# First guess of the inverse root in the stream norms: VectorE's reciprocal and a ScalarE square root in place of logarithm and exponential

## Chip, cores and metric

The kernel runs on one core of a Trainium2 chip. The metric is the device time of one execution in microseconds (us), lower is better. The time of the kernel before is the median of three runs, and its profile is one further execution.

## What is computed

Two transformer blocks follow each other on 512 tokens of width 1024, in fp32. The first has a gated feed-forward layer (ffn1), a mixer of gated linear attention and convolution (mix), a cross attention to a memory of 256 tokens (xat) and a second feed-forward layer (ffn2), and ends in a norm. The second adds 16 meta tokens (528 in all) and has a latent attention (mla), a feed-forward layer with convolution (cffn0), a pooling mixer (pool) and another such layer (cffn1). Ahead of each layer, and behind each of the second block, stands an RMS norm over the width:

```python
def rms_norm(x, g):
    xf = x.astype(jnp.float32)
    y = xf * lax.rsqrt(jnp.mean(xf * xf, axis=-1, keepdims=True) + EPS)
    return (y * g.astype(jnp.float32)).astype(x.dtype)
```

The change touches how `rsqrt` of that mean is found for twelve of these norms.

## The kernel before

The activations X lie with the width on the 128 partitions, as eight tiles of 128 x tokens. A weight matrix is read in units: a unit is up to eight tiles of 128x128, which SP loads (`raw`), ScalarE rounds into a high part (`w_hi`, L490), and GpSimd subtracts into a low part (`w_lo`, L477). PE multiplies the unit in three passes (L544 w_hi by high part of X, L546 w_hi by its low part, L548 w_lo by its high part) into one of four pairs of PSUM banks. There are four raw slots and two of w_hi and w_lo, so `w_hi` of unit n+2 waits until PE is through with unit n, and PE waits for the two halves of `w_lo` of its unit.

Each engine runs a program written out by hand in one order; semaphores join them, and there is no planner. A norm is made so. ScalarE squares the tiles (L639). They are summed over the tiles either on PE, which multiplies each by ones (`pe_square`, L566), or on VectorE (`acc`, L654) with one multiplication by ones at the end (`pe_norm`, L559). Every partition then holds the sum for every token, so the rest is work on a 128 x tokens tile (512, 516 or 528 tokens):

- VectorE, `dve_norm`: L688 scales and adds EPS, out of PSUM into `ms`, and signals `norm_ms`.
- ScalarE, `act_sqrt`: waits for `norm_ms`, then `act_rsqrt`: `sd = Ln(ms)` at L670, `sd = Exp(-0.5 sd)` at L671, signals `norm_sd`. Ahead of an activation whose table is not loaded stands an ACT_TABLE_LOAD, put down to the activation's line.
- VectorE waits for `norm_sd` and does one Newton step in three instructions (`newton`, L675 to L677), which gives `rn`.

`sd` and the scratch `rt` are slices of `post_t`, which is the name that the rows show. In `dve_norm` and `newton` `link` makes VectorE wait for its own last write.

```python
    def newton(link, r, v, t, s, last=None):
        link(nc.vector.tensor_tensor(t, s, s, ALU.mult))
        link(nc.vector.scalar_tensor_tensor(t, t, -0.5, v, ALU.mult, ALU.mult))
        (last or link)(nc.vector.scalar_tensor_tensor(r, t, 1.5, s, ALU.add, ALU.mult))
```

Twelve norms go through `act_sqrt` and `dve_norm`, here called by their places: FFN1, MIX, XAT, FFN2 (ahead of the layers of the first block), FIN (its end), MLA, MLAP (ahead of and behind the latent attention), CF0, CF0P, POOL, POOLP and CF1 (likewise around cffn0, pool and cffn1). Seven of them (FFN1, MIX, XAT, FFN2, MLA, CF0, CF1) stand ahead of a layer whose first product does not need `rn`: the weights are multiplied by X scaled by the gain alone, and `rn` comes in when the product is read out of PSUM (L903 in `dve_ffn`). PE goes on with units 1, 2 and 3 in that time; before unit 3 it waits for `norm_ms`, since that unit's PSUM pair held the sum. The other five (FIN, MLAP, CF0P, POOL, POOLP) make values that the next product needs (`dve_post`, L959 and L963: X plus the normed output; L1716; L2340 for the pool).

ScalarE's order at a feed-forward layer is: `w_hi` of unit 2, `act_sqrt`, then the first activations of the layer, then `w_hi` of unit 3. Eight further inverse roots (four in the mixer, one of the memory, two of the latent attention, one at the output) call `act_rsqrt` directly.

Of the kernel before, what the change touches and what calls it, by code (L numbers as in the profile page):

```python
# [17 lines left out]
ALU = mybir.AluOpType  # L18
ACT = mybir.ActivationFunctionType
# [3 lines left out]
D = 1024  # L23
# [12 lines left out]
EPS = 1e-6  # L36
# [106 lines left out]
def program(nc, ctx, A, out):  # L143
    def sb(name, shape, dt=F32, scope=ctx):
        return scope.enter_context(nc.sbuf_tensor(name, shape, dt))

    def sem(name):
        return ctx.enter_context(nc.semaphore(name))
# [12 lines left out]
    ms = sb("ms", [P, S2 + 8])  # L161
    rn = sb("rn", [P, S2 + 8])
    post_t = sb("post_t", [P, 3, S2 + 8])
    rt, sd = post_t[:, 0, :], post_t[:, 1, :]
# [125 lines left out]
    norm_ms = sem("norm_ms")  # L290
    norm_sd = sem("norm_sd")
# [213 lines left out]
    def psv(pair, blk):  # L505
        return PS[pair][:, 0, :] if blk == 1 else PS[pair][:, :, 0:width(blk) // 2]

    def sv(ap, blk):
        return ap if blk == 1 else ap.rearrange("p (c w) -> p c w", c=2)

    def width(blk):
        return (S1, S2, S3)[blk - 1]
# [142 lines left out]

    def act_sqrt(act, s, w):
        act.wait_ge(norm_ms, s + 1)
        act_rsqrt(act, sd[:, 0:w], ms[:, 0:w]).then_inc(norm_sd, 1)

    act_steps = [0]  # L660

    def act_link(act, ins):

        act_steps[0] += 1
        ins.then_inc(act_step, 1)
        act.wait_ge(act_step, act_steps[0])

    def act_rsqrt(act, dst, v):

        act_link(act, nc.scalar.activation(dst, v, ACT.Ln))  # L670
        return nc.scalar.activation(dst, dst, ACT.Exp, scale=-0.5)  # L671
# [7 lines that stand above are left out]
    def dve_norm(dve, link, s, pair, blk, rc=0):  # L679

        w = width(blk)
        if s in PE_SUMMED:
            dve.wait_ge(acc_done, KD * (s + 1))
        else:
            dve.wait_ge(norm_sum, len([x for x in range(s + 1) if x not in PE_SUMMED]))
        if rc:
            link(nc.vector.tensor_scalar(ms[:, w:w + rc], PS[pair][:, 1, 0:rc], 1.0 / D, EPS, ALU.mult, ALU.add))
        nc.vector.tensor_scalar(sv(ms[:, 0:w], blk), psv(pair, blk), 1.0 / D, EPS, ALU.mult, ALU.add).then_inc(norm_ms, 1)  # L688
        dve.wait_ge(norm_sd, s + 1)
        w += rc  # L690
        newton(link, rn[:, 0:w], ms[:, 0:w], rt[:, 0:w], sd[:, 0:w])

    def gain_of(name, index):
# [130 lines left out]
    def act_ffn(act, name, blk, inv, s, after):  # L824
# [4 lines left out]
        for pi, (f0, nt) in enumerate(PARTS):  # L829
# [9 lines left out]
            def up(it, n=n, pi=pi, f0=f0, count=count):  # L839
                for a in range(2):  # L840
                    g = (inv * FT + f0 + a) + 2 * it
                    soon = blk > 1 and first(it) and pi == 0 and a == 0
                    look(it, n, 2 * a, count)
                    if first(it) and pi == 0 and a == 0:
                        act_sqrt(act, s, w)
                    act.wait_ge(unit_read, later(n, it, 2 * a + 1))
                    if blk > 1:
                        f = (f0 + a) + 2 * it
                        nc.scalar.activation(g_conv[:, 0:w], g_buf[:, 2:2 + w], ACT.Identity, scale=tap(inv - 2, 2, f),  # L849
                                             bias=tap(inv - 2, 3, f)).then_inc(conv_tap, 1)  # L850
                        if soon:
                            look(it, n, 2 * a + 1, count)
                        act.wait_ge(conv_done, (2 * (cb + f0 + a) + 1) + 4 * it)
                        nc.scalar.activation(g_act[:, 0:w], g_conv[:, 0:w], ACT.Silu).then_inc(silu_done, 1)
                    else:
                        nc.scalar.activation(g_act[:, 0:w], g_buf[:, 0:w], ACT.Silu).then_inc(silu_done, 1)
                    if not soon:
                        look(it, n, 2 * a + 1, count)
                    if blk > 1:
                        act.wait_ge(unit_read, later(n, it, 2 * a + 2))  # L860
                        nc.scalar.activation(u_conv[:, 0:w], u_buf[:, 2:2 + w], ACT.Identity, scale=tap(inv - 2, 2, f + FT),  # L861
                                             bias=tap(inv - 2, 3, f + FT)).then_inc(conv_tap, 1)
                    act.wait_ge(hid_prod, g + 1)
                    nc.scalar.activation(h_hi[:, a + 2 * it, 0:w], hid[:, 0:w], ACT.Copy).then_inc(hid_hi, 1)  # L864
# [19 lines left out]
    def dve_ffn(dve, link, name, blk, inv, s, after):  # L884
# [3 lines left out]
        if blk > 1:  # L888
            link(nc.vector.memset(g_buf[:, 0:2], 0.0))
            link(nc.vector.memset(u_buf[:, 0:2], 0.0))  # L890
        dve_norm(dve, link, s, (n + 3) % 4, blk)
        r = sv(rn[:, 0:w], blk)
        n_down = None
# [59 lines left out]
    def dve_post(dve, link, i, s, n, gain, d_next=None, g_next=None, blk_next=2):  # L953
        dve_norm(dve, link, s, n % 4, 2)
        for k in range(KD + 3):
            if k < KD:
                if k >= 3:
                    dve.wait_ge(post_added, KD * i + k - 2)
                nc.vector.scalar_tensor_tensor(post_t[:, k % 3, 0:S2], M[:, k, :], gain(k), rn[:, 0:S2], ALU.mult,  # L959
                                               ALU.mult).then_inc(post_scaled, 1)  # L960
            if 1 <= k <= KD:
                dve.wait_ge(post_scaled, KD * i + k)
                nc.vector.tensor_tensor(X[:, k - 1, :], X[:, k - 1, :], post_t[:, (k - 1) % 3, 0:S2],  # L963
                                        ALU.add).then_inc(post_added, 1)
            if k >= 3 and d_next is not None:
                dve_split(dve, d_next, k - 3, blk_next, g_next)

    def act_post(act, i, s, s_next, d_next=None, g_next=None, blk_next=2):
        act_sqrt(act, s, S2)
        for k in range(KD):  # L970
            act.wait_ge(post_added, KD * i + k + 1)
            if d_next is not None:
                act_split(act, d_next, k, k, blk_next, g_next)
            act_square(act, s_next, k, k, xt(k, blk_next), width(blk_next))
# [232 lines left out]
    def act_mixer(act):  # L1207
# [3 lines left out]
        act.dma_start(gate_w[0:16, 0:256], A["gate_fwd_w"][0]).then_inc(small_in, 16)  # L1211
        act.dma_start(gate_w[16:32, 256:512], A["gate_bwd_w"][0]).then_inc(small_in, 16)
        act_sqrt(act, S_MIX, S1 + 4)
        hi_to(act, n + 4)
        pe_mix.wait(act, "lg")
# [96 lines left out]
    def dve_mixer(dve, link):  # L1312
# [9 lines left out]
        dve.wait_ge(unit_summed, n)  # L1322
        dve_mix.inc(nc.vector.memset(gate_w[:, :], 0.0), "gz")
        dve_norm(dve, link, S_MIX, (n + 3) % 4, 1, rc=4)
        nc.vector.tensor_tensor(zz[:, :], summed(0)[0:32, :], R[0:32, :], ALU.mult).then_inc(unit_read, 1)
        for t in range(2):
# [1160 lines left out]
```

## Time and profile before

| what | value |
| --- | --- |
| median of three runs | 2468.05 us (2458.19 to 2468.3) |
| the profiled execution: its time, and its span | 2468.25 us, 2466.5 us |
| busy: PE, VectorE, ScalarE, GpSimd | 94%, 43%, 37%, 40% |
| instructions of PE, VectorE, ScalarE | 14099, 1584, 1656 |
| L670 and L671, ACT_TABLE_LOAD | 20 and 20, 25.7 us each |

The span is from the first to the last instruction; the execution's own time has 1.75 us beside it. PE is busy nearly throughout, so time is won or lost where it stands still: such a place is read from the idle time ahead of an instruction of PE's timeline and the engine that ended it.

### The profile page before, as it was taken

To read this page: it belongs to the slowest core of one execution; us is meant where nothing else is said; L and a number is where in the kernel's file an instruction comes from. 1 tells how busy PE (TensorE), PEld (TensorE's weight loads), DVE (VectorE), ACT (ScalarE), POOL (GpSimd) and SP (SyncE) were. 2 spreads that over 40 slices of the span, in tenths; PEclk is the share of its full clock that TensorE was granted. 3 is DMA by queue.
4 is the path that set the end of the run, shared out by engine and by line. 5 is a ranking of instruction groups with operands and counts; after the bars stand their busy time and mean duration, and the time that the engine had idled before them with its cause. 6 is when DMAs were issued, how large, how long until landed. Compare 5 with 4: busy or idle time off the path is not lost.

```text
span 2466.5 us, 35997 instructions
## 1 busy us (share of the span) xinstructions
PE 2308.9 (94%) x14099; PEld 2027.3 (82%) x14099; DVE 1069.0 (43%) x1584; ACT 910.1 (37%) x1656; POOL 998.1 (40%) x758
## 2 busy tenths in 40 slices
PE   8999999999889899999988999799999938999999
PEld 6888887777677678888877888799999837999999
DVE  3313134564432242231356563562644475626354
ACT  4323235313353342222354453542433335424243
POOL 3445454532363344444531112244444432444443
PEclk9999999998899999999999999899999968999999
DMA  4333323321242123333211011133232201333221
GB/s 145 94 97 95 94 81 91 86 69 35 86 137 69 52 84 96 94 94 94 86 56 32 28 35 49 48 93 94 86 94 84 79 9 57 89 94 94 86 88 67
DMA packets 355686, 193.61 MB, mean 78 GB/s; under 512 B 7357, under 2 KB 350034, under 8 KB 355554
## 3 DMA queue, kind: packets, MB, share of 16 engines
q1 hardware_dynamic: 355026, 190.61, 26.4%
q8 instruction: 90, 1.47, 0.2%
q10 hardware_dynamic: 528, 1.19, 0.2%
q14 instruction: 42, 0.34, 0.0%
HBM read 189.67 MB, written 2.10 MB: 78 GB/s over the span
## 4 chain that ended last, share of the span: by engine, by line
PE 82%; DVE 11%; ACT 4%; issue 2%; DMA 0%; DVEq 0%; ACTq 0%; SPq 0%; POOL 0%
PE PS L544 22%; PE PS L546 22%; PE PS L548 22%; PE PS L1966 2%; PE PS L566 2%; PE PS L1984 1%; DVE u_conv L908 1%; PE PS L2038 1%; PE PS L2020 1%; ACT w_hi L490 1%; DVE g_conv L908 1%; PE PS L1155 1%; DVE hid L919 1%; PE PS L1567 1%; DVE u_conv L911 1%
## 5 line engine op out<-in xcount | busy, mean ns | idle before, releaser
L477 POOL TENSOR_TENSOR w_lo<-raw,w_hi 128x512 fp32r<-128x512 f32 (+4 forms) x743 | 976.4, 1336 | 1417.9 <-ACT w_hi L490 1417.9
L544 PE MATMUL PS<-XHI,w_hi 128*128 128x512 f32 (+2 forms) x2632 | 741.8, 332 | 41.0 <-DVE XLO L644 37.0
L490 ACT ACTIVATE w_hi<-raw 128x512 fp32r<-128x512 f32 (+4 forms) x743 | 412.5, 604 | 943.4 <-PE PS L548 879.4
L546 PE MATMUL PS<-XLO,w_hi 128*128 128x512 f32 (+2 forms) x2632 | 731.6, 328 | 0.0
L548 PE MATMUL PS<-XHI,w_lo 128*128 128x512 f32 (+2 forms) x2632 | 729.0, 327 | 0.0
L544 PEld LDWEIGHTS PS<-XHI,w_hi 128*128 128x128 f32 x2632 | 446.8, 190 | 97.4 <-issue 45.2
L546 PEld LDWEIGHTS PS<-XLO,w_hi 128*128 128x128 f32 x2632 | 444.7, 190 | 46.3 <-issue 2.9
L548 PEld LDWEIGHTS PS<-XHI,w_lo 128*128 128x128 f32 x2632 | 445.0, 190 | 43.6
L544 PE MATMUL PS<-h_hi,w_hi 128*128 128x512 f32 (+2 forms) x1056 | 282.3, 321 | 5.9 <-DVE h_lo L921 5.8
L546 PE MATMUL PS<-h_lo,w_hi 128*128 128x512 f32 (+2 forms) x1056 | 281.6, 321 | 0.0
L548 PE MATMUL PS<-h_hi,w_lo 128*128 128x512 f32 (+2 forms) x1056 | 281.5, 321 | 0.0
L544 PEld LDWEIGHTS PS<-h_hi,w_hi 128*128 128x128 f32 x1056 | 174.9, 188 | 23.7 <-issue 6.3
L546 PEld LDWEIGHTS PS<-h_lo,w_hi 128*128 128x128 f32 x1056 | 175.7, 189 | 16.1
L548 PEld LDWEIGHTS PS<-h_hi,w_lo 128*128 128x128 f32 x1056 | 175.1, 188 | 15.3
L903 DVE TENSOR_TENSOR u_buf<-PS,rn 128x512 f32<-128x512 f32 (+2 forms) x88 | 61.2, 695 | 229.7 <-PE PS L548 229.7
L864 ACT ACTIVATE h_hi<-hid 128x512 fp32r<-128x512 f32 (+5 forms) x88 | 56.0, 636 | 207.6 <-DVE hid L919 207.6
L903 DVE TENSOR_TENSOR g_buf<-PS,rn 128x512 f32<-128x512 f32 (+2 forms) x88 | 61.1, 694 | 99.2 <-PE PS L548 99.1
L936 DVE SCALAR_TENSOR_TENSOR X<-PS,X 128x512 f32<-128x512 f32 x48 | 33.2, 691 | 160.6 <-PE PS L548 160.6
L921 DVE TENSOR_TENSOR h_lo<-hid,h_hi 128x512 f32 (+5 forms) x88 | 68.9, 783 | 73.7 <-ACT h_hi L864 73.7
L908 DVE SCALAR_TENSOR_TENSOR u_conv<-u_buf,cols,u_conv 128x528 f32<-128x528 f32 (+1 forms) x44 | 71.4, 1622 | 65.7 <-ACT u_conv L861 65.7
L908 DVE SCALAR_TENSOR_TENSOR g_conv<-g_buf,cols,g_conv 128x528 f32<-128x528 f32 (+1 forms) x44 | 55.0, 1251 | 47.4 <-ACT g_conv L849 47.4
L2088 ACT ACTIVATE pt<-PS 128x640 f32<-128x640 f32 (+4 forms) x80 | 37.4, 472 | 87.0 <-PE PS L2020 86.1
(294 smaller groups left out, 2404.3 us busy)
## 6 DMA issues: line engine op xcount, KB each, us to landing
raw<-in_ffn_w_up SPq DMA_DIRECT2D x132, 512.0 KB, 3.7
raw<-in_ffn_w_down SPq DMA_DIRECT2D x64, 512.0 KB, 3.8
raw<-in_ffn_w_gate SPq DMA_DIRECT2D x44, 512.0 KB, 3.8
raw<-in_w_in SPq DMA_DIRECT2D x25, 512.0 KB, 3.7
raw<-in_ffn_w_down SPq DMA_DIRECT2D x32, 384.0 KB, 3.4
raw<-in_xattn_w_kv SPq DMA_DIRECT2D x16, 512.0 KB, 3.7
raw<-in_w_out SPq DMA_DIRECT2D x8, 512.0 KB, 3.7
raw<-in_xattn_w_q SPq DMA_DIRECT2D x8, 512.0 KB, 4.4
```

What stands on the lines that cost most here:

```text
L477: ins = nc.gpsimd.tensor_tensor(d, r, h.bitcast(F32), ALU.subtract)
L490: ins = nc.scalar.activation(d, r, ACT.Copy)
L544: nc.tensor.matmul(ps, wh, ahi(k)[:, c:c + w], start=(k == 0), stop=False)
L546: nc.tensor.matmul(ps, wh, alo(k)[:, c:c + w], start=False, stop=False)
L548: ins = nc.tensor.matmul(ps, wl, ahi(k)[:, c:c + w], start=False, stop=(k == u.kt - 1))
L566: ins = nc.tensor.matmul(ps, ones, sq[:, k % 2, c:c + w], start=(k == 0), stop=(k == KD - 1))
L864: nc.scalar.activation(h_hi[:, a + 2 * it, 0:w], hid[:, 0:w], ACT.Copy).then_inc(hid_hi, 1)
L903: nc.vector.tensor_tensor(sv(dst, blk), psv(m % 4, blk), r, ALU.mult).then_inc(unit_read, 1)
L908: nc.vector.scalar_tensor_tensor(cv_[:, 0:w], buf[:, 1:1 + w], tap(inv - 2, 1, ft), cv_[:, 0:w], ALU.mult, ALU.add).then_inc(conv_mid, 1)
L921: nc.vector.tensor_tensor(h_lo[:, a + 2 * it, 0:w], hid[:, 0:w], h_hi[:, a + 2 * it, 0:w].bitcast(F32), ALU.subtract).then_inc(hid_lo, 1)
L1966: ins = nc.tensor.matmul(bank[:, 0:CW], w, x[:, k, c * CW:(c + 1) * CW], start=st, stop=sp_)
L2088: act_m.inc(nc.scalar.activation(pt[:, x % 4, 0:j + 1, 0:nq], turn_at(x).rearrange("p (i q) -> p i q", q=P)[:, :, 0:nq], ACT.Copy), ("tc", x))
```

## The change

In `dve_norm` VectorE now follows the scaling at L688 with a reciprocal of `ms` into `sd`, and `norm_ms` is signalled by the reciprocal. In `act_sqrt` ScalarE takes the square root of `sd` in place, with one activation (L658), in place of `act_rsqrt`. The Newton step stays. The eight direct calls of `act_rsqrt` stay. Behind L655 lines shift by up to one, so L903 is now L904.

```diff
     def act_sqrt(act, s, w):
         act.wait_ge(norm_ms, s + 1)
-        act_rsqrt(act, sd[:, 0:w], ms[:, 0:w]).then_inc(norm_sd, 1)
+        nc.scalar.activation(sd[:, 0:w], sd[:, 0:w], ACT.Sqrt).then_inc(norm_sd, 1)
@@ dve_norm
         if rc:
             link(nc.vector.tensor_scalar(ms[:, w:w + rc], PS[pair][:, 1, 0:rc], 1.0 / D, EPS, ALU.mult, ALU.add))
-        nc.vector.tensor_scalar(sv(ms[:, 0:w], blk), psv(pair, blk), 1.0 / D, EPS, ALU.mult, ALU.add).then_inc(norm_ms, 1)
+        link(nc.vector.tensor_scalar(sv(ms[:, 0:w], blk), psv(pair, blk), 1.0 / D, EPS, ALU.mult, ALU.add))
+        w += rc
+        nc.vector.reciprocal(sd[:, 0:w], ms[:, 0:w]).then_inc(norm_ms, 1)
         dve.wait_ge(norm_sd, s + 1)
-        w += rc
         newton(link, rn[:, 0:w], ms[:, 0:w], rt[:, 0:w], sd[:, 0:w])
```

The order of instructions on ScalarE at the norms MLAP and CF0, of the kernel before (`XHI` is the high part of X, `sq` a squared tile; the eight pairs L633, L639 between the two norms are cut to the first). At MLAP:

```order
L639 ACTIVATE sq<-M 128x528
L670 ACT_TABLE_LOAD
L670 ACTIVATE post_t<-ms 128x528
L671 ACT_TABLE_LOAD
L671 ACTIVATE post_t<-post_t 128x528
L633 ACTIVATE XHI<-X,cols 128x528
```

At CF0:

```order
L490 ACTIVATE w_hi<-raw 128x512 x2
L670 ACT_TABLE_LOAD
L670 ACTIVATE post_t<-ms 128x528
L671 ACT_TABLE_LOAD
L671 ACTIVATE post_t<-post_t 128x528
L849 ACTIVATE g_conv<-g_buf,cols 128x528
```

The same two places in the changed kernel, MLAP first:

```order
L639 ACTIVATE sq<-M 128x528
L658 ACT_TABLE_LOAD
L658 ACTIVATE post_t<-post_t 128x528
L633 ACTIVATE XHI<-X,cols 128x528
```

```order
L490 ACTIVATE w_hi<-raw 128x512 x2
L658 ACTIVATE post_t<-post_t 128x528
L850 ACTIVATE g_conv<-g_buf,cols 128x528
```

The load and the activation between `ms` and the result are gone, and the second of two such norms in a row has no load at all. Over the whole program ScalarE has 48 table loads before and 33 after; two are new, ahead of the first exponential of the mixer's gates (L1226) and of the cross attention's softmax (L1611).

VectorE at MLAP in the changed kernel:

```order
L688 TENSOR_SCALAR ms<-PS 128x528
L690 RECIPROCAL post_t<-ms 128x528
L675 TENSOR_TENSOR post_t<-post_t 128x528
L676 SCALAR_TENSOR_TENSOR post_t<-post_t,ms 128x528
L677 SCALAR_TENSOR_TENSOR rn<-post_t 128x528
```

The reciprocal of the whole tile is new and stands behind L688, at all twelve norms; nothing else moves. PE, GpSimd and SP have the same instructions in the same order.

## Rows read from the trace of the kernel before

**Rows 1.** The page: span, and the chain that ended last, by engine.
```profile
span 2466.5 us, 35997 instructions
...
PE 82%; DVE 11%; ACT 4%; issue 2%; DMA 0%; DVEq 0%; ACTq 0%; SPq 0%; POOL 0%
```

**Rows 2.** PE's timeline at five norms: start us, length us, what [idle before <- releaser].
```profile
1254.27 0.56 PE L544 MATMUL PS<-XHI,w_hi 128*128 128x264 f32 x1 [8.01 <-DVE XLO L644]
1567.94 0.78 PE L544 MATMUL PS<-XHI,w_hi 128*128 128x264 f32 x2 [11.12 <-DVE XLO L644]
1979.59 0.78 PE L566 MATMUL PS<-sq,const 128*128 128x264 f32 x1 [8.52 <-ACT sq L639]
2018.28 0.56 PE L2259 MATMUL PS<-XHI,w_hi 128*128 128x264 f32 x1 [28.39 <-DVE XLO L2345]
2054.86 0.55 PE L544 MATMUL PS<-XHI,w_hi 128*128 128x258 f32 x1 [11.24 <-DVE XLO L644]
```

**Rows 3.** VectorE's timeline, the first Newton step of those five norms, same columns.
```profile
1249.63 0.69 DVE L675 TENSOR_TENSOR post_t<-post_t 128x512 f32<-128x512 f32 x1 [2.64 <-ACT post_t L671]
1974.47 0.71 DVE L675 TENSOR_TENSOR post_t<-post_t 128x528 f32<-128x528 f32 x1 [2.66 <-ACT post_t L671]
1993.36 0.71 DVE L675 TENSOR_TENSOR post_t<-post_t 128x528 f32<-128x528 f32 x1 [2.66 <-ACT post_t L671]
2047.16 0.71 DVE L675 TENSOR_TENSOR post_t<-post_t 128x528 f32<-128x528 f32 x1 [2.80 <-ACT post_t L671]
```

**Rows 4.** ScalarE's and VectorE's timelines at the norm behind the latent attention (MLAP).
```profile
1554.71 1.28 ACT L670 ACT_TABLE_LOAD   x1
1557.60 0.64 ACT L670 ACTIVATE post_t<-ms 128x528 f32<-128x528 f32 x1 [1.61 <-DVE ms L688]
1558.26 1.28 ACT L671 ACT_TABLE_LOAD   x1
1559.55 0.64 ACT L671 ACTIVATE post_t<-post_t 128x528 f32<-128x528 f32 x1
...
1556.86 0.71 DVE L688 TENSOR_SCALAR ms<-PS 128x528 f32<-128x528 f32 x1 [1.31 <-PE PS L559]
1560.23 0.71 DVE L675 TENSOR_TENSOR post_t<-post_t 128x528 f32<-128x528 f32 x1 [2.66 <-ACT post_t L671]
```

**Rows 5.** Groups of VectorE instructions, shapes kept apart: count, busy us, mean ns.
```profile
L675 DVE TENSOR_TENSOR post_t<-post_t 128x528 f32<-128x528 f32 x7 | 5.0, 708 | 17.9 <-ACT post_t L671 17.8
L675 DVE TENSOR_TENSOR post_t<-post_t 128x4 f32<-128x4 f32 x1 | 0.2, 151 | 0.0
L2167 DVE RECIPROCAL mst<-mst 128x1 f32<-128x1 f32 x80 | 12.5, 156 | 5.3 <-ACT pr L2079 4.3
L1679 DVE RECIPROCAL xst<-xst 128x1 f32<-128x1 f32 x16 | 2.5, 153 | 0.0
L919 DVE TENSOR_TENSOR hid<-g_act,u_buf 128x512 f32<-128x512 f32 x44 | 63.9, 1453 | 4.9 <-ACT g_act L856 0.3
```

**Rows 6.** Timelines at the latent norm (MLA): ScalarE, VectorE, GpSimd.
```profile
1280.99 1.15 ACT L490 ACTIVATE w_hi<-raw 128x512 fp32r<-128x512 f32 x2 [0.72 <-PE PS L548]
1273.48 0.71 DVE L675 TENSOR_TENSOR post_t<-post_t 128x528 f32<-128x528 f32 x1 [3.56 <-ACT post_t L671]
1278.32 2.54 POOL L477 TENSOR_TENSOR w_lo<-raw,w_hi 128x512 fp32r<-128x512 f32 x2 [6.69 <-ACT w_hi L490]
```

**Rows 7.** The same three engines at the first norm of the program (FFN1).
```profile
44.26 1.15 ACT L490 ACTIVATE w_hi<-raw 128x512 fp32r<-128x512 f32 x2 [1.81 <-PE PS L548]
37.34 0.69 DVE L675 TENSOR_TENSOR post_t<-post_t 128x512 f32<-128x512 f32 x1 [3.59 <-ACT post_t L671]
41.48 3.06 POOL L477 TENSOR_TENSOR w_lo<-raw,w_hi 128x512 fp32r<-128x512 f32 x2 [5.96 <-ACT w_hi L490]
```

**Rows 8.** Timelines in the mixer's gates: ScalarE, then VectorE.
```profile
426.07 1.91 ACT L1227 ACTIVATE t<-t 128x2048 f32<-128x2048 f32 x1
433.15 0.69 DVE L1334 TENSOR_TENSOR ks<-PS,rn 128x512 f32<-128x512 f32 x1 [4.87 <-PE PS L548]
```

## The prediction

> **What bounds the kernel now.** I read the chain that ended last first [rows 1]: 82% of the span of 2466.5 us is PE, 11% VectorE, 4% ScalarE. So a norm costs time only where PE stands still for it. The twelve norms differ in that, and PE's timeline sorts them. At five of them (FIN, MLAP, CF0P, POOL, POOLP) PE is idle for 8.01, 11.12, 8.52, 28.39 and 11.24 us, and what ends it is a tile made from `rn` [rows 2]: the whole way from the sum to `rn` lies in that idle time, so each microsecond put on it or taken off is one of the span. At the other seven PE works on units that do not need `rn`.
>
> In the first case the way is seen whole at MLAP [rows 4]. VectorE's scaling of `ms` ends at 1557.57. ScalarE's first table was loaded from 1554.71 on, ahead of its wait, and costs nothing. The logarithm runs at 1557.60 for 0.64 us, the second table load at 1558.26 for 1.28, the exponential at 1559.55 for 0.64, and the first Newton step starts at 1560.23. So VectorE waits 2.66 us. At the other exposed norms it waits 2.64 (FIN), 2.66 (CF0P), 2.66 (POOL) and 2.80 us (POOLP, where ScalarE comes a little late) [rows 3]. The five sum to 13.42 us.
>
> **Part 1, what goes and what stays on the exposed way.** In place of those waits stand a reciprocal of length R and a square root. I price the square root as the logarithm, 0.64 us for the same tile, and each of the three hand-overs (`ms` to reciprocal, reciprocal to square root, square root to Newton step) at 0.03, the gap between 1557.57 and 1557.60 [rows 4]. Its table load, where there is one, falls ahead of the wait as the first one did, and is free; if the wait came first it would still lie under R unless R were below 1.28. So each exposed norm has R + 0.73 us, five have 3.65 us and five times R. The change returns 13.42 - 3.65 = 9.77 us and pays five reciprocals. It breaks even at R of about 1.95.
>
> Of the table loads, these rows show 1.28 us each and the next activation 0.01 behind [rows 4]. The Trainium skill (ScalarE: Activation LUTs, section What ACT_TABLE_LOAD costs) puts a switch at 1283 ns and a drain of some 1380 ns more. The load agrees, the drain is not in the rows; by the page each of the five would return 1.38 us more, and the sum below would be some 7 us lower, about 2472. I go by the rows.
>
> **Part 2, R.** No row has a reciprocal of a wide tile. From below: one element a tick. A Newton step takes 708 ns for 528 elements and 151 for 4 [rows 5], so 1.063 ns an element on a base of 147, and R would be 0.69 us at 512 and 0.71 at 528. From above: the two groups of reciprocals of one element take 153 and 156 ns [rows 5], and a Newton step of one element would take 148. If those 5 to 8 ns were paid for every element, an element would cost 6.06 to 9.06 ns, and R at 528 would be 3.35 to 4.93 us. But 5 to 8 ns may also be paid once an instruction. I take the slow reading: the excess is five to eight ticks of the 1.063 ns on a single element, and both groups show it. Within it I take the middle, 7.56 ns, as the two rows pull equally: R = 4.02 us at 512 elements (FIN) and 4.14 at 528 (the other four). The ends kept for the range are 0.69/0.71 and 4.79/4.93.
>
> Sum of the exposed norms: 4.02 + 4 x 4.14 = 20.58, less 9.77: **+10.8 us**.
>
> **Part 3, the covered norms.** PE waits for the signal `norm_ms` ahead of unit 3, and ScalarE reaches `w_hi` of unit 3 only behind the layer's first activations, so that unit is what comes late. At MLA VectorE waits 3.56 us now, as ScalarE first makes `w_hi` of unit 2 and has both tables to load [rows 6]; then it is R + 0.73, 4.87, so all behind it is 1.3 us later. The first half of `w_lo` of unit 3 is ready at 1278.32 + 1.27 = 1279.6. Unit 3 starts at 1280.99, when the end of unit 2 frees a slot for the next `w_hi` [rows 6]. The slack is 1.4: covered, barely. At FFN1 the wait goes from 3.59 to 4.75, 1.2 later, against 44.26 - (41.48 + 1.53) = 1.25 of slack [rows 7]. FFN2, CF0 and CF1 are built like these two, and I take them as covered too. If R is small nothing is gained here, since PE was not waiting. At MIX and XAT `rn` is needed only when a product is read out, and PE has three more units to run. `norm_ms` itself comes R later, but more than 10 us ahead of unit 3. Sum: 0, but 0.1 to 0.75 a place if R is above my value.
>
> **Part 4, two new table loads.** One stands ahead of the mixer's gate exponential. The gates' last ScalarE step of that stretch ends at 426.07 + 1.91 = 427.98, and VectorE takes up its result only behind work that starts at 433.15 [rows 8]; 1.28 us of 5 is covered. If that cover were gone it would cost 1.28. The other stands ahead of the first softmax exponential, where ScalarE waits for scores. It costs 0 to 1.28; I take 0, as a load needs no operand and can run in the wait.
>
> **Forecast.** 2468.25 us, the profiled execution's own time, + 10.8 = 2479. The median of the runs is 2468.05, so the two stand alike. This is +0.44%, and within the 0.5% (12.3 us) that a measurement of this kernel can tell from no change.
>
> **Rival A, slower: each element of a reciprocal takes eight ticks, and the covered norms come uncovered.** In the group of 156 ns the one element has 8 ns over the 148 of a Newton step, some eight ticks. Eight times 1.063 ns is 8.5 ns an element, R = 4.50 and 4.64. The exposed norms give 4.50 + 4 x 4.64 - 9.77 = +13.3. At MLA the delay is 1.8 against 1.4 of slack, at FFN1 1.64 against 1.25, so PE stalls some 0.4 us at each of five places, +2.0. Time 2483.5. It decides from R above about 4.2, when the stalls begin. For it speaks the 156 ns row with 80 instances; against it the 153. The Trainium skill (VectorE: DVE Perf Modes, section First, the fixed hardware budget) says that a reciprocal is an iterated divide on two slices "with a repeat count of 8"; if that is eight ticks an element, this rival is what it gives. The trace has only one-element reciprocals and cannot settle it.
>
> **Rival B, a little faster: one element a tick.** R = 0.69 and 0.71, five of them 3.53, less 9.77: -6.2, time 2462. For it speaks that every other arithmetic row on VectorE runs so, and that instructions differ by 10 ns in their base anyway. This is also what the change needs to pay off. Even then it stays within 0.5%.
>
> **Rival C, contention or a wait of its own.** At FFN1, FFN2, MLA, CF0 and CF1 GpSimd works on `w_lo` of unit 2 during the reciprocal. Products of two SBUF tiles beside GpSimd take 1453 ns where a Newton step takes 708 [rows 5]. If the reciprocal stretched by as much, 0.75 us, or held GpSimd up, each of the five would stall PE for about that. With both new loads exposed, 2.6, that is 10.8 + 3.7 + 2.6 = +17, time 2485. Against it: a reciprocal reads one tile, not two.
>
> **Chances.** Forecast (slow, 6 to 8 ns an element) 0.40, A 0.27, B 0.26, C 0.07. Over 12.3 us slower are most of A (0.2), nearly all of C (0.06) and the upper tenth or two of the forecast's case (0.08): 0.34. Faster by over 12.3 us needs twice what the best R gives; only scatter of the runs, which spans 10 us already, reaches it: 0.05. Within: 0.61. The range goes from just under B, 2460, to the high end of R: 4.79 + 4 x 4.93 = 24.5, less 9.77 = +14.7, with some 0.65 stall at each of the five places +18, so 2487.
>
> **What would show it.** L690 at 512 and 528 elements gives R at once. VectorE's wait ahead of L675 at MLAP should be about 0.7 us, between the end of the reciprocal and the Newton step. PE's idle times at the five places should each grow by R - 1.93 (POOLP R - 2.07). PE should show no new idle time near unit 3 of the covered layers if R is below 4.2. ScalarE should have 33 table loads, none between `ms` and the square root. The forecast is wrong if R lies outside 3.3 to 4.6, or if the idle times of PE move by something other than R foretells, which would mean a load or a hand-over that I count as free.

## The result, and the profile after

Six runs of the changed kernel have a median of 2475.26 us (2474.56 to 2478.03), six of the kernel before 2461.6 (2458.19 to 2468.3). The ratio is 1.0052, with a 95% interval from 1.0038 to 1.0065: 12.8 us slower (9.4 to 16.0). That lies on the bound of 0.5% that the prediction set for "no change". The profiled execution of the changed kernel took 2475.47 us, 7.2 more than the profiled one before. The later runs of the kernel before show that its first profile was a long draw (below), so 12.8 is the number to explain, not 7.2.

The page of the changed kernel, its span, busy times and the chain by engine:

```profile
span 2473.7 us, 35982 instructions
PE 2307.9 (93%) x14099; PEld 2027.3 (82%) x14099; DVE 1110.4 (45%) x1596; ACT 883.2 (36%) x1629; POOL 998.8 (40%) x758
...
PE 82%; DVE 12%; ACT 3%; issue 2%; DMA 0%; DVEq 0%; ACTq 0%; SPq 0%; POOL 0%
```

ScalarE lost 27 us of work, VectorE gained 41, PE's busy time is the same within 1 us. The 41 us are the twelve reciprocals, in VectorE's groups with shapes kept apart:

```profile
L690 DVE RECIPROCAL post_t<-ms 128x528 f32<-128x528 f32 x6 | 20.7, 3453 | 0.2
L690 DVE RECIPROCAL post_t<-ms 128x512 f32<-128x512 f32 x4 | 13.4, 3353 | 0.1
...
L690 DVE RECIPROCAL post_t<-ms 128x516 f32<-128x516 f32 x2 | 6.8, 3379 | 0.1
```

So R is 3.35 us at 512 elements and 3.45 at 528, some 6.25 ns an element, against 4.02 and 4.14 in the forecast. The way at MLAP, which stands in [rows 4] for the kernel before, on ScalarE's and then VectorE's timeline:

```profile
1552.36 1.28 ACT L658 ACT_TABLE_LOAD   x1
1558.74 0.64 ACT L658 ACTIVATE post_t<-post_t 128x528 f32<-128x528 f32 x1 [5.10 <-DVE post_t L690]
...
1554.51 0.71 DVE L688 TENSOR_SCALAR ms<-PS 128x528 f32<-128x528 f32 x1 [1.31 <-PE PS L559]
1555.25 3.45 DVE L690 RECIPROCAL post_t<-ms 128x528 f32<-128x528 f32 x1
1559.41 0.71 DVE L675 TENSOR_TENSOR post_t<-post_t 128x528 f32<-128x528 f32 x1 [0.71 <-ACT post_t L658]
```

The load stands ahead of the wait, the square root takes 0.64 us, and VectorE waits 0.71 for it. From the end of `ms` (1555.22) to the Newton step it is 4.19 us, where it was 2.66. PE's idle times at the five exposed norms, which answer to [rows 2]:

```profile
1249.77 0.78 PE L544 MATMUL PS<-XHI,w_hi 128*128 128x264 f32 x2 [9.46 <-DVE XLO L644]
1567.13 0.78 PE L544 MATMUL PS<-XHI,w_hi 128*128 128x264 f32 x2 [12.66 <-DVE XLO L644]
1984.21 0.78 PE L566 MATMUL PS<-sq,const 128*128 128x264 f32 x1 [10.06 <-ACT sq L639]
2024.20 0.56 PE L2260 MATMUL PS<-XHI,w_hi 128*128 128x264 f32 x1 [29.92 <-DVE XLO L2346]
2060.66 0.77 PE L544 MATMUL PS<-XHI,w_hi 128*128 128x258 f32 x2 [12.64 <-DVE XLO L644]
```

They grew by 1.45, 1.54, 1.54, 1.53 and 1.40 us, 7.5 in all, which is what five reciprocals of this length give: 3.35 + 4 x 3.45 = 17.2, less 9.77. The other 5.3 us are somewhere else.

### The profile page after: what moved, and what is told of

The parts are those of the page before. It is cut to its first block, busy times and chain, and to the rows that moved or that the text cites. A ratio compares the mean times of both kernels' runs of the same rounds, so it can differ in the third digit from the quotient of the medians.

```text
span 2473.7 us, 35982 instructions
## 1 busy us (share of the span) xinstructions
PE 2307.9 (93%) x14099; PEld 2027.3 (82%) x14099; DVE 1110.4 (45%) x1596; ACT 883.2 (36%) x1629; POOL 998.8 (40%) x758
## 4 chain that ended last, share of the span: by engine, by line
PE 82%; DVE 12%; ACT 3%; issue 2%; DMA 0%; DVEq 0%; ACTq 0%; SPq 0%; POOL 0%
PE PS L544 22%; PE PS L546 22%; PE PS L548 22%; PE PS L566 2%; PE PS L1967 2%; PE PS L1985 1%; DVE u_conv L909 1%; PE PS L2021 1%; PE PS L2039 1%; DVE post_t L690 1%; ACT w_hi L490 1%; DVE g_conv L909 1%; PE PS L1156 1%; DVE hid L920 1%; DVE u_conv L912 1%
## 5 line engine op out<-in xcount | busy, mean ns | idle before, releaser
L904 DVE TENSOR_TENSOR u_buf<-PS,rn 128x512 f32<-128x512 f32 (+2 forms) x88 | 61.1, 695 | 229.5 <-PE PS L548 229.5
L904 DVE TENSOR_TENSOR g_buf<-PS,rn 128x512 f32<-128x512 f32 (+2 forms) x88 | 61.0, 693 | 98.2 <-PE PS L548 98.1
```

Of the source, the lines that this page charges most:

```text
L904: nc.vector.tensor_tensor(sv(dst, blk), psv(m % 4, blk), r, ALU.mult).then_inc(unit_read, 1)
```

## Where the rest of the time lies

To find it I cut the executions at the starts of L688, the instruction that ends each norm's sum. Each number is the difference of two such starts on VectorE's timeline, in us; "before 2" is a second profile of the kernel before (2464.57 us), from a run told of below, as are the other columns. The last two rows have the whole from FIN on, and the time of it in which PE is busy.

| stretch | before | before 2 | changed | exposed only | covered only | CF0, CF1 only | one activation |
| --- | --- | --- | --- | --- | --- | --- | --- |
| start to FIN | 1246.3 | 1242.5 | 1240.3 | 1240.2 | 1242.3 | 1244.3 | 1238.7 |
| FIN to MLA | 22.9 | 22.8 | 25.2 | 25.2 | 22.8 | 22.9 | 21.8 |
| MLA to MLAP | 287.7 | 288.5 | 289.0 | 289.4 | 288.4 | 288.5 | 289.2 |
| MLAP to CF0 | 26.2 | 25.8 | 28.5 | 28.3 | 25.9 | 25.8 | 24.9 |
| CF0 to CF0P | 388.0 | 388.2 | 391.2 | 388.0 | 389.6 | 390.1 | 387.2 |
| CF0P to POOL | 18.9 | 18.5 | 20.2 | 20.0 | 18.3 | 19.3 | 17.0 |
| POOL to POOLP | 53.7 | 53.6 | 53.7 | 53.7 | 52.1 | 53.7 | 50.2 |
| POOLP to CF1 | 26.7 | 26.5 | 27.3 | 27.2 | 26.7 | 26.9 | 24.0 |
| CF1 to the end | 396.1 | 396.2 | 398.3 | 396.2 | 396.7 | 397.1 | 394.5 |
| FIN to the end | 1220.2 | 1220.2 | 1233.3 | 1228.0 | 1220.6 | 1224.4 | 1208.9 |
| of it PE busy | 1119.8 | 1119.6 | 1125.6 | 1120.2 | 1120.1 | 1122.5 | 1121.9 |

Up to FIN the kernels differ by 8 us with no relation to their edits, and the two profiles of one kernel by 3.8. Of that 0.6 us lie ahead of FFN1, 1.5 between MIX and XAT and 1.7 between XAT and FFN2. (From MIX to the mixer's first own root the first profile has 188.3 us and the second 183.2, but the first makes 3.7 of these up before the next root.) That is why the first profile was long. From FIN to the end the two profiles of the kernel before agree within 0.1 us, and the changed kernel has 13.1 more. So the whole loss lies there. PE has the same instructions there, yet is busy 5.9 us longer, and its idle time has grown by 7.2 us (from 100.5 to 107.7). The loss is more than the growth of the five idle times in two ways.

First, the layers behind CF0 and CF1, which I had counted as covered, are 3.0 and 2.1 us longer. Second, FIN to MLA is 2.4 us longer and MLAP to CF0 2.3 to 2.7, where the idle times grew by 1.45 and 1.54. One stretch gave something back: POOL to POOLP is as long as before though its idle time grew by 1.53, as PE's next wait there fell from 2.29 to 1.69 us and its products ran at a higher mean clock (0.88 where 0.85 was granted; PE is busy for 22.0 us there and was for 22.9). What both ways have in common is shown by the clock.

## The experiments

Each kernel was timed beside runs of the kernel before, except the last. Where a difference in us is given, it is the ratio's distance from 1 times 2462 us, with the interval in brackets.

### The exposed and the covered norms apart

The edit, shown against the changed kernel, with the norms FIN, MLAP, CF0P, POOL and POOLP in the set, or the other seven (the guard in `dve_norm` is told in words):

```diff
 def act_sqrt(act, s, w):
     act.wait_ge(norm_ms, s + 1)
-    nc.scalar.activation(sd[:, 0:w], sd[:, 0:w], ACT.Sqrt).then_inc(norm_sd, 1)
+    if s in SET:
+        nc.scalar.activation(sd[:, 0:w], sd[:, 0:w], ACT.Sqrt).then_inc(norm_sd, 1)
+    else:
+        act_rsqrt(act, sd[:, 0:w], ms[:, 0:w]).then_inc(norm_sd, 1)
@@ dve_norm: the reciprocal only where s in SET
```

> The new route at the five exposed norms alone (FIN, MLAP, CF0P, POOL, POOLP), the old one at the other seven. Theory 1, only the way to rn counts: the reciprocals measured in the changed kernel, 3.353 us at 512 elements and 3.453 at 528, sum to 17.2 us; less the 9.77 us that the route returns that is +7.4 us over the kernel before, 2469 on its median of 2461.6. Theory 2, longer idle times also cost PE low clock behind them: +11 to +14, as in the changed kernel.

Measured: ratio 1.0030, +7.4 us (4.4 to 10.6). That is theory 1's number, and theory 2's 11 to 14 us lie outside the interval. The profile has 7.8 us more from FIN on, nearly all of it idle time of PE (its busy time there is 0.5 us longer): lower clock added some behind FIN and MLAP, and POOL to POOLP gave as much back.

> The new route at the seven covered norms alone (FFN1, MIX, XAT, FFN2, MLA, CF0, CF1). Theory 1: 0 us, at most +0.5 (the changed kernel shows PE idle 0.2 us near unit 3 of CF0 and CF1). Theory 2: 0 too, since no idle time grows by more than that. Rival: if the later start of VectorE's work in these layers is what cost the part beyond 7.4 us, it shows here, +3 to +6.

Measured: ratio 1.0020, +4.9 us (2.7 to 7.4), an interval without 0. The two add up to 12.3, close to the 12.8 of both together, so by the times the missing 5 us come from norms that I had called covered, and theory 1 as I had put it falls. The profile of this kernel does not show them all the same. From FIN on it has 1220.6 us, only 0.4 more than the kernel before: the layers behind CF0 and CF1 are 1.5 and 0.6 us longer, and POOL to POOLP is 1.5 shorter. So that covered norms cost something is shown by the times; how the 5 us are shared out is read from the other profiles, and in part stays open.

### Which of the covered norms

The same edit with smaller sets.

> The new route at CF0 and CF1 alone. The kernel with all seven covered norms was 4.9 us (2.7 to 7.4) slower where 0 to 0.5 was expected. Theory A: it comes from these two. VectorE's work in the convolution layers has no slack between the norm and the end of the first part, where PE waits for h_lo (1.64 and 1.70 us before, 1.88 in that kernel), and PE idles 0.2 us more near unit 3; 0.8 us of idle in all, and low clock behind it: +2 to +4 us. Theory B, the new table loads or the other five: 0 to +0.8 here.

Measured: ratio 1.0013, +3.2 us (0.2 to 5.9).

> The new route at MIX and XAT alone, where it brings the two new table loads ahead of an exponential (48 loads as before). Theory A: 0 us. Theory B: the new loads are exposed, +1.3 to +2.6 us.

Measured: ratio 0.9999, -0.2 us (-3.2 to 2.5).

> The new route at FFN1, FFN2 and MLA alone. Theory A: 0 us, the stretch between FFN1 and MIX stays at 371.0 us and that behind FFN2 at 366.7 as in all kernels so far with one reciprocal. A rival with stalls at the units would give +0.4 each, +1.2.

Measured: ratio 0.9995, -1.2 us (-4.4 to 2.0); the stretch from FFN1 to MIX is 371.0 us in it and in the kernel before alike, and that behind FFN2 366.7.

The intervals are as wide as the effects, and the three kernels sum to 1.8 us where the seven norms at once cost 4.9, so the times alone do not share the loss out. The table of stretches sides with theory A: with CF0 and CF1 alone the stretches behind them are 390.1 and 397.1 us, 2.0 and 1.0 more than before, and no other stretch from FIN on moves by more than 0.8. Here is PE's timeline in the changed kernel in the layer behind CF0, at unit 4 and at the first product that needs `h_lo`:

```profile
1600.69 0.39 PE L544 MATMUL PS<-XHI,w_hi 128*128 128x264 f32 x1 [0.20 <-POOL w_lo L477]
...
1680.61 0.48 PE L544 MATMUL PS<-h_hi,w_hi 128*128 128x264 f32 x2 [1.88 <-DVE h_lo L922]
1680.93 0.41 PE L546 MATMUL PS<-h_lo,w_hi 128*128 128x264 f32 x2
...
1682.42 0.64 PE L544 MATMUL PS<-h_hi,w_hi 128*128 128x264 f32 x2
1682.87 0.64 PE L546 MATMUL PS<-h_lo,w_hi 128*128 128x264 f32 x2
...
1685.65 0.40 PE L548 MATMUL PS<-h_hi,w_lo 128*128 128x264 f32 x2
```

And in the kernel before:

```profile
1680.02 0.48 PE L544 MATMUL PS<-h_hi,w_hi 128*128 128x264 f32 x2 [1.64 <-DVE h_lo L921]
...
1682.55 0.41 PE L546 MATMUL PS<-h_lo,w_hi 128*128 128x264 f32 x2
```

The wait for `h_lo` grew from 1.64 to 1.88 us, and unit 4 has a new one of 0.20. That is 0.4 us. But some 1.5 us behind the longer wait the same pair of products takes 0.64 us instead of 0.41, for 3 us. The stretches 1670 to 1680.6 and 1682 to 1685 of the changed kernel, and 1670 to 1680 and 1682 to 1685 of the kernel before (length, busy times, then PE's granted clock, DMA share and GB/s):

```profile
1670.00:1680.60 10.60, 8.73 (x72) 8.54 (x71) 6.72 (x7) 3.42 (x6) 3.83 (x4) 1.00 0.33 99
1682.00:1685.00 3.00, 3.00 (x15) 3.00 (x15) 0.34 (x1) 1.11 (x2) 2.33 (x2) 0.50 0.01 3
```

```profile
1670.00:1680.00 10.00, 8.38 (x69) 8.18 (x68) 6.64 (x7) 3.05 (x5) 3.24 (x3) 1.00 0.35 105
1682.00:1685.00 3.00, 3.00 (x27) 3.00 (x26) 0.31 (x1) 0.49 (x2) 2.34 (x2) 1.00 0.03 5
```

In the changed kernel PE ran at the lower of its two levels, 1.2 GHz, and finished 15 products where the kernel before finished 27. It had been idle for 1.88 us shortly before, in the kernel before for 1.64. Behind CF1 it looks the same: a wait of 1.91 us instead of 1.71, and pairs of products of 0.63 us from 2173.34 to 2176.4. So in this profile a delay of 0.7 us at the norm is followed by some 1.5 us of lost clock behind each of the two. (The stretch behind CF0 is 3.0 us longer: 0.7 of delay, 1.5 here, and most of the rest in its last 2.3 us, which run at a granted clock of 0.50.)

The longer wait does not bring the lower clock each time. The kernel with the covered norms alone has the same waits, 1.88 us behind CF0 and 1.89 behind CF1, and its products 1.4 us behind them run at the full clock:

```profile
1677.01 0.48 PE L544 MATMUL PS<-h_hi,w_hi 128*128 128x264 f32 x2 [1.88 <-DVE h_lo L929]
...
1678.40:1681.40 3.00, 3.00 (x27) 3.00 (x26) 0.34 (x1) 0.84 (x2) 2.54 (x2) 1.00 0.00 0
```

Over the profiles of all kernels told of here, this wait behind CF0 or CF1 was 1.75 us or less nine times, and the clock did not fall behind it once. It was 1.88 to 2.28 us nine times, and at five of these some 3 us at 1.2 GHz followed or had just begun (both places in the changed kernel, both with each reciprocal twice, and CF0 in the kernel with CF0 and CF1 alone), and at four not (one of them with the old route at CF1). So the fall goes with the longer wait, and what else decides it is not shown. It also means that the changed kernel's two falls, 3 us, are not a fixed price of the change.

The same lower level makes FIN to MLA and MLAP to CF0 about 1 us longer than the idle time explains. From the start of PE's wait at MLAP to the end of the first unit behind it, in the changed kernel and in the one before:

```profile
1554.40:1582.10 27.70, 15.04 (x79) 13.62 (x79) 22.61 (x31) 10.91 (x17) 0.00 (x0) 0.69 0.07 20
```

```profile
1556.82:1582.20 25.38, 14.26 (x78) 13.06 (x79) 18.98 (x30) 12.84 (x19) 0.00 (x0) 0.73 0.08 21
```

The same unit keeps PE busy for 15.04 us instead of 14.26, at a mean granted clock of 0.69 instead of 0.73.

### A reciprocal that costs one tick an element

The reciprocal is replaced by a subtraction on the bits of `ms`, a rough guess of the reciprocal, so the norms come out less exact:

```diff
-        nc.vector.reciprocal(sd[:, 0:w], ms[:, 0:w]).then_inc(norm_ms, 1)
+        nc.vector.tensor_scalar(sd[:, 0:w].bitcast(int32), ms[:, 0:w].bitcast(int32), -1.0, float(0x7EF311C3),
+                                ALU.mult, ALU.add).then_inc(norm_ms, 1)
```

> The changed kernel with the reciprocal replaced at all twelve norms by an integer subtraction on the bits of ms, one element a tick, which gives only a rough reciprocal, so the norms come out less exact. Theory 1: R falls to 0.7 us, so -6.2 us against the kernel before. Theory 2: -6 to -10, as shorter idle times also return clock. If the reciprocal's length were not what made the change slower, this kernel would stay above the one before.

Measured: ratio 0.9989, -2.7 us (-5.4 to -0.2). The sign turned, so it is the length of the reciprocal that made the change slower. The gain is less than 6.2, and two places account for most of it. At FIN VectorE's timeline, and GpSimd's below it:

```profile
1243.88 3.21 DVE L690 TENSOR_SCALAR post_t<-ms 128x512 int32<-128x512 int32 x1
...
1243.52 3.30 POOL L2320 MEMSET pr<- 128x3840 f32 x1
```

The subtraction, 0.43 us for the 528 elements of MLAP (0.7 was expected), took 3.21 here, and it ended 0.3 us after a memset of GpSimd that had begun before it. So this norm gained nothing (PE's idle time there is 9.32 us, 1.31 more than before). At POOLP it took 1.16, beside `w_lo`:

```profile
2040.09 1.16 DVE L690 TENSOR_SCALAR post_t<-ms 128x528 int32<-128x528 int32 x1
...
2038.46 2.49 POOL L477 TENSOR_TENSOR w_lo<-raw,w_hi 128x512 fp32r<-128x512 f32 x2 [2.18 <-ACT w_hi L490]
```

All twelve keep to this. The four with GpSimd idle (XAT, MLAP, CF0P, POOL) took 0.43 or 0.44 us. The eight that began during an instruction of GpSimd took 0.65 to 3.21 us, and each ended 0.28 or 0.29 us after the one that was running. A reciprocal beside the same memset in the changed kernel is not stretched:

```profile
1241.07 3.35 DVE L690 RECIPROCAL post_t<-ms 128x512 f32<-128x512 f32 x1
...
1240.71 3.29 POOL L2319 MEMSET pr<- 128x3840 f32 x1
```

At MLAP, CF0P and POOL the idle times fell by 1.48 us each, as they should, at POOLP by 0.89. Behind CF0 and CF1 the waits of 1.64 and 1.71 us went below 0.1. That also shows that these two norms had never been covered, though the layers did not save all of it: they are 0.7 and 1.7 us shorter.

### Each reciprocal twice

```diff
+        link(nc.vector.reciprocal(rt[:, 0:w], ms[:, 0:w]))
         nc.vector.reciprocal(sd[:, 0:w], ms[:, 0:w]).then_inc(norm_ms, 1)
```

> The changed kernel with each reciprocal done twice, the first into scratch. Exposed norms: +7.4 and five more of 3.46, +24.7 us over the kernel before. Covered norms: at MLA VectorE's wait would go from 3.56 to 7.66 us against 1.4 us of slack, so PE should now stall 2.5 to 3 us at each of five, +13. Theory 1: +37 in all. Theory 2: +42 to +50.

Measured: ratio 1.0228, +56 us (53 to 60), more than either theory. PE's waits in this kernel, by releaser:

```profile
PE PS L544 <- DVE XLO L644: 52.5, 5, 16.1
PE PS L2261 <- DVE XLO L2347: 35.1, 2, 33.4
PE PS L544 <- POOL w_lo L477: 15.5, 8, 3.0
PE PS L566 <- ACT sq L639: 13.5, 1, 13.5
```

The exposed waits grew by 24.8 us (at MLAP 16.14 us, 5.02 more than before), as expected. The waits for `w_lo`, which the kernel before does not have at these places, are 15: 2.7 us each at FFN1 and FFN2, 3.0 at MLA, and 2.7 or 2.5 and then 0.8 at CF0 and CF1 (the eighth of the row, 0.4 us, is in the mixer). So the slack at FFN1, FFN2 and MLA is what the prediction read (at FFN1 two reciprocals and 0.76 us are 7.47, less the old wait of 3.59 and 1.25 of slack is 2.63, and 2.68 came). Together they are 40 us. Of the other 16, slower products account for some 9: PE is busy 5.3 us longer from FIN on, and the layers behind FFN1 and FFN2 are 5.7 and 3.9 us longer for 2.7 us of wait each. The mean granted clock of the span is 0.961 where the kernel before has 0.968. The rest is not placed.

### A guess in one activation

The reciprocal is left out, and ScalarE's function for the inverse root of the absolute value takes the place of logarithm and exponential, with the Newton step as it was:

```diff
     def act_sqrt(act, s, w):
         act.wait_ge(norm_ms, s + 1)
-        act_rsqrt(act, sd[:, 0:w], ms[:, 0:w]).then_inc(norm_sd, 1)
+        nc.scalar.activation(sd[:, 0:w], ms[:, 0:w], ACT.Abs_reciprocal_sqrt).then_inc(norm_sd, 1)
```

> The kernel before with one ScalarE activation, the inverse root of the absolute value, in place of logarithm and exponential at the twelve norms, with no work added on VectorE; the Newton step stays. The wait at an exposed norm is 0.03 + 0.64 + 0.03 = 0.70 us in place of 2.64 to 2.80: -9.9 us. If VectorE's chain in the convolution layers has no slack (theory A), the idle 1.64 and 1.70 us ahead of the second product there go too: -13.2 in all, 2449. If that idle time has another cause: -9.9, 2452. A table of its own that costs more than 1.28 us to load would show at POOLP.

Measured: ratio 0.9948, -12.8 us (-17.5 to -8.1), median 2450.07 us. It is faster than both kernels. MLAP on VectorE's and ScalarE's timelines:

```profile
1549.77 0.71 DVE L688 TENSOR_SCALAR ms<-PS 128x528 f32<-128x528 f32 x1 [1.31 <-PE PS L559]
1551.19 0.71 DVE L675 TENSOR_TENSOR post_t<-post_t 128x528 f32<-128x528 f32 x1 [0.71 <-ACT post_t L658]
...
1547.62 1.28 ACT L658 ACT_TABLE_LOAD   x1
1550.52 0.64 ACT L658 ACTIVATE post_t<-ms 128x528 f32<-128x528 f32 x1 [1.61 <-DVE ms L688]
```

The wait of 2.66 us is 0.71, and its table load too stands ahead of the wait. PE's idle times at the exposed norms fell by 9.8 us in all, and its waits of 1.64 and 1.71 us for `h_lo` behind CF0 and CF1 have gone, so the idle time that theory A named is gone in full. The interval of the times holds both -13.2 and -9.9, so it is the profile that decides for theory A. From FIN to the end it has 1208.9 us, 11.3 less than before: idle time fell by 13.5 and the products took 2.2 longer, part of it between MLA and MLAP, which is about 1 us longer.

### The same at all twenty inverse roots

```diff
     def act_rsqrt(act, dst, v):
-        act_link(act, nc.scalar.activation(dst, v, ACT.Ln))
-        return nc.scalar.activation(dst, dst, ACT.Exp, scale=-0.5)
+        return nc.scalar.activation(dst, v, ACT.Abs_reciprocal_sqrt)
```

> The single activation of e8_one_activation at all twenty inverse roots, the eight direct calls too. The kernel before has the logarithm and exponential of the memory's norm on the chain (two loads, ahead of an idle time of PE) and four roots of the mixer one behind the other, each with two loads of 1.28 us: VectorE paces that chain with 4.1 us a root, so it may give only the first wait. I expect 3 to 8 us below e8_one_activation, so -16 to -21 against the kernel before, 2443 to 2448. If the eight direct calls are all covered, the time is that of e8_one_activation.

Measured: ratio 0.9966, -8.4 us (-11.6 to -4.9), runs from 2447.51 to 2459.33. The further gain isn't there. Its profile (2447.51 us, span 2445.7) is 1.9 us shorter than that of the kernel with one activation at twelve norms, its median (2455.03 us) 5.0 higher, and the intervals of the two overlap, so whether the eight direct calls give anything, or cost something in the scattering stretches of the mixer, stays open. VectorE paces the mixer's four roots, as expected: 4.16 us from one Newton step to the next, as in the kernel before.

### The kernel before once more

> The kernel before once more, unchanged, for a second profile of it. If the mixer's stretch of 188.3 us and its low clock in the first profile are scatter, it is 183 to 185 us here, and the stretches behind the norms CF0 and CF1 stay within 1 us of 388.0 and 396.1.

One run, 2464.57 us. The stretch from MIX to the mixer's first own root is 183.2 us, and those behind CF0 and CF1 are 388.2 and 396.2: as expected. Between these two profiles the difference lies ahead of FIN.

## Why the prediction was right, and where it was not

The time, 2475.3 us, lies inside the range of 2460 to 2487 and is near 2479; the loss of 12.8 us is near the 10.8 of the forecast. It stands on the bound between "within 0.5%" and "slower", and the measurement doesn't say on which side. But that the sum came near is luck, through errors of opposite sign. R was 3.3 us too high in the sum, the covered norms and the clock, 5.3 us, were put at nothing, and the forecast started from an execution of 2468.25 us where the median of the kernel before is 2461.6. From that median its own +10.8 gives 2472.4, 2.9 below what was measured.

- **Part 1 held.** The returned 9.77 us and the 0.73 beside R were right within a tenth: the five idle times grew by 7.5 us with R as measured, and the exposed norms alone cost 7.4. No drain stands behind the table loads that were on the way, nor in front of the square root, where the Trainium skill (ScalarE: Activation LUTs, section What ACT_TABLE_LOAD costs) counts some 1380 ns a switch. The trace disagrees with that part. By the rule the change would have returned 7 us more, and the exposed norms alone would have cost 0.6; they cost 7.4.
- **Part 2, R, was too high.** The step was to take the middle of the excess of 5 to 8 ns an element. The measured 6.25 ns an element is near the low end, 6.06, which the row of 153 ns gives. The slow reading was right, and the term should have been +7.5 where the forecast has +10.8. ("Five to eight ticks" was loose: 5 to 8 ns are 4.7 to 7.5 of them.) The repeat count of 8 of the Trainium skill (VectorE: DVE Perf Modes, section First, the fixed hardware budget) was rival A's; eight ticks an element would be 4.50 us at 512, and 3.35 was measured, some six ticks. So the trace does not bear that reading out.
- **Part 3 was wrong at CF0 and CF1.** I looked for the late part at unit 3 and its slack of 1.4 us, and took CF0 and CF1 to be built like MLA and FFN1. Unit 3 is not late in any kernel with one reciprocal. The sign that I had set for it, no new idle time while R is below 4.2, did not hold. For in the convolution layers ScalarE reaches `w_hi` of unit 4 only behind the first hidden tile (L864), and VectorE works without slack from the norm to the last `h_lo` of the first part, so that each delay appears there: 0.2 and 0.2 us of idle time at CF0, 0.2 and 0.2 at CF1, with slower products behind in the changed kernel. Alone the two cost 3.2 us (0.2 to 5.9), all seven covered norms 4.9 (2.7 to 7.4); whether the other five have a share in that is open. The chain that ended last in the kernel before did run through VectorE's work in these layers.
- **The clock was left out.** The sum counted idle time alone. From FIN on PE is busy 5.9 us longer with the same instructions: about 1 us each at FIN and MLAP, some 1.5 us behind each of CF0 and CF1, and the rest in between. At CF0 and CF1 this does not come with every profile of so long a wait.
- **Part 4 held.** The two new loads with their norms cost -0.2 us (-3.2 to 2.5).
- **Rival B** would have given 2462; the kernel with the cheap guess shows its mechanism, -2.7 instead of -6.2. **Rival C** did not come: twelve reciprocals have the same length for their shapes, beside GpSimd (eight) or not (four). But the argument that I gave against it, one tile read and not two, is no rule: the subtraction of the cheap guess reads one tile as well, and it was stretched at all eight.

## What to carry to other kernels

Before an operation of unknown length is put on a path that PE waits for, price it from its smallest instances: the excess of one element over a plain instruction of one element, times the elements, came within 3% of the measured length by one of the two rows, and 43% above it by the other, 3 ns apart. So a few nanoseconds in the smallest instance decide, and one instance at full width should be timed. A step is covered only if each later place that its delay reaches has slack; the chain of waits shows where it hasn't. And a replacement should first be sought that makes the operation unnecessary: one activation in place of two gave 12.8 us where moving half of the work to VectorE lost as much.

## What the runs showed of the hardware that I had not expected

- An integer subtraction on VectorE took 0.43 us for 528 elements with GpSimd idle. Begun during an instruction of GpSimd (a memset, or the making of `w_lo`) it ended 0.3 us after that instruction each of eight times, after up to 3.21 us. A reciprocal in the same places kept its 3.35 to 3.46 us.
- An idle time of PE of 1.88 to 2.28 us was followed by some 3 us of products at 1.2 GHz in five of nine places, one of 1.75 us or less in none of nine.
- ScalarE's inverse root in one activation takes 0.64 us for 128x528, as long as logarithm, exponential or square root on that tile, and needs one table load, ahead of the wait.
